# Five norms of a two-layer trunk: two units of weights multiplied before the root is known

## What is computed

```python
h = modulate(rms_norm(x), sh, sc)      # x * rsqrt(mean(x*x) + EPS) * (1 + sc) + sh
x = x + 0.5 * g[:, None, :] * swiglu(h, w_gu, w_down)   # or g * mixer(h)
def swiglu(h, w_gu, w_down):
    g, u = jnp.split(h @ w_gu, 2, axis=-1)
    return (jax.nn.silu(g) * u) @ w_down
```

## Times and profile before

| | us |
|---|---|
| median of 3 runs | 2059.26 (2059.01 to 2061.18) |
| the profiled execution | 2060.86 |
| its span | 2059.1 |
| PE, matmuls | 2019.0 busy, 98% of the span |
| PE, weight loads | 1668.5, 81% |
| DVE | 1084.0, 53% |
| ACT | 683.8, 33% |
| POOL | 185.3, 9% |

### The profile page before, as it was taken

One profiled execution on the slowest core, in us unless ns is written; L12 is line 12 of the kernel. 1 busy time (PEld: TensorE's weight loads), 2 busy tenths in 40 slices (PEclk: granted clock), 3 DMA queues, 4 the chain that ended last, 5 costly groups with the idle time before them and its releaser, 6 DMA issues.

```text
span 2059.1 us, 23630 instructions
## 1 busy us (share of the span) xinstructions
PE 2019.0 (98%) x9290; PEld 1668.5 (81%) x9290; DVE 1084.0 (53%) x1642; ACT 683.8 (33%) x986; POOL 185.3 (9%) x216
## 2 busy tenths in 40 slices
PE   6999999999999999999999999999999999999998
PEld 5888888788888888887888888878888878888886
DVE  7665653579746655635654553365455453433334
ACT  5222222344633322224222221345454443222122
POOL 3110100016600101000110000000000000000000
PEclk9999999999999999999999999999999999999999
DMA  8665642322035656523454542221222123322321
GB/s 325 230 212 173 201 145 70 95 86 72 21 103 173 205 172 203 184 85 95 147 189 137 164 153 92 72 93 60 74 71 62 52 82 102 103 92 92 102 87 57
DMA packets 72014, 253.98 MB, mean 123 GB/s; under 512 B 8025, under 2 KB 8153, under 8 KB 71938
## 3 DMA queue, kind: packets, MB, share of 16 engines
q1 hardware_dynamic: 53280, 185.62, 27.7%
q0 software_dynamic: 18512, 67.26, 10.0%
q10 hardware_dynamic: 146, 0.09, 0.0%
HBM read 250.70 MB, written 2.10 MB: 123 GB/s over the span
## 4 chain that ended last, share of the span: by engine, by line
PE 93%; DVE 4%; ACT 1%; issue 1%; POOL 1%; ACTq 0%; DVEq 0%; POOLq 0%
PE bank L1125 28%; PE bank L1130 28%; PE bank L1126 28%; PE bank L1187 1%; PE bank L1136 1%; DVE arena L951 1%; DVE top L950 1%; PE bank L1501 1%; PE bank L1538 1%; PE bank L1430 1%; PE bank L1271 1%; DVE wlo L665 1%; PE bank L1273 1%; PE bank L1272 0%; PE bank L1489 0%
## 5 line engine op out<-in xcount | busy, mean ns | idle before, releaser
L1125 PE MATMUL bank<-h_hi,whi 128*128 128x512 f32 x1808 | 711.0, 393 | 9.5 <-DVE wlo L665 4.5
L1126 PE MATMUL bank<-h_hi,wlo 128*128 128x512 f32 x1808 | 705.8, 390 | 0.0
L1130 PE MATMUL bank<-h_lo,whi 128*128 128x512 f32 x1808 | 589.6, 391 | 0.5 <-POOL h_lo L311 0.5
L382 ACT ACTIVATE whi<-wraw 128x1024 fp32r<-128x1024 f32 x338 | 346.8, 1055 | 269.1 <-PE bank L1130 266.1
L665 DVE TENSOR_TENSOR wlo<-wraw,whi 128x1024 fp32r<-128x1024 f32 x325 | 390.2, 1224 | 55.7 <-ACT whi L382 54.2
L1125 PEld LDWEIGHTS bank<-h_hi,whi 128*128 128x128 f32 x1808 | 340.8, 188 | 83.9 <-issue 11.0
L1130 PEld LDWEIGHTS bank<-h_lo,whi 128*128 128x128 f32 x1808 | 338.9, 188 | 75.2 <-DVE h_lo L740 3.4
L1126 PEld LDWEIGHTS bank<-h_hi,wlo 128*128 128x128 f32 x1808 | 340.8, 189 | 69.7
L1130 PE MATMUL bank<-hid_lo,whi 128*128 128x512 f32 x832 | 324.3, 390 | 3.2 <-DVE hid_lo L793 3.2
L788 DVE TENSOR_TENSOR dve_tmp<-act_tmp,bank 128x512 f32<-128x512 f32 x88 | 60.6, 689 | 504.3 <-ACT act_tmp L429 504.2
L1125 PE MATMUL bank<-hid_hi,whi 128*128 128x512 f32 x832 | 324.6, 390 | 0.0
(11 more groups left out here) (207 smaller groups left out, 1348.7 us busy)
## 6 DMA issues: line engine op xcount, KB each, us to landing
wraw<-in_w_units_dram SPq DMA_DIRECT2D x306, 512.0 KB, 3.5
arena<-in_mod_t_dram POOLq DMA_DIRECT2D x96, 512.0 KB, 4.9
mod_tile<-in_mod_t_dram POOLq DMA_DIRECT2D x32, 512.0 KB, 4.6
wraw<-in_w_units_dram SPq DMA_DIRECT2D x32, 384.0 KB, 3.3
arena<-in_mod_t_dram SPq DMA_DIRECT2D x12, 512.0 KB, 7.9
xT<-in_xt_dram SPq DMA_DIRECT2D x8, 256.0 KB, 4.0
out_dram<-xT SPq DMA_DIRECT2D x8, 256.0 KB, 2.2
mod_tile<-in_mod_t_dram SPq DMA_DIRECT2D x2, 512.0 KB, 9.5
```

The costliest lines, as they stand in the source:

```text
L382: act.activation(whi[:, s % RING, :, :], wraw[:, s % RING, :, :], ACT.Copy).then_inc(hi_ready, 1)
L1125: pe.matmul(dst, whi[:, w, k, :], hi_, start=first, stop=False)
L1126: pe.matmul(dst, wlo[:, w, k, :], hi_, start=False, stop=False)
L1130: return pe.matmul(dst, whi[:, s % RING, k, :], lo_, start=False, stop=last)
```

## The change

Behind each of the five norms the first two units no longer read h. They read the scaled residual x (1 + sc), split into the same `h_hi` and `h_lo`, made by ACT and DVE in `down_stats` as each xT[d] is ready. PE's new `early` runs these two units one after the other, with the sums of squares behind the fourth k-step of the first, the spread of the root behind its eighth (norm 3: the second spread behind the fourth k-step of the second unit), and two more matmuls in each k-step: the weight tile's high and low part by the shift, split in two columns (`shift_split`), into bank 5. ACT copies the spread root from RB to `ssum`. DVE's `take_early` sums the parts of sh W, multiplies both units' banks by the root into `sq`, and the shift enters as a bias or scalar at the next instruction. h itself is made as before, but each piece overwrites the scaled residual's only when the second unit has used it, and is read from the third unit on. All fillers at the five norms are gone; the last norm's stay. In FoX the forget sums and the bias matmuls move behind head 0's first work, and the layer-0 final scaling of xT (`post_first`) moves into FFN 2. The core of the diff:

```diff
+            def round_h(st, s):
+
+                v, sh, _ = modulation(st)
+                act.wait_ge(rb_ready, RB_BEFORE[v])
+                act.activation(ssum[:, :], bank[RB], ACT.Copy).then_inc(rb_kept, 1)
                 for k in range(KT):
+                    if k == 3:
+                        hi(s + 4)
+                    if k == 7:
+                        hi(s + 5)
+                    act.wait_ge(early_used, KT * (v - 1) + k + 1)
...
+                            if early and q == 0:
+                                act.wait_ge(evicted, s + 1)
+                                act.activation(act_tmp[:, 0, :], sq[:, 0, :], ACT.Silu, bias=shift_out[:, 0:1],
+                                               scale=1.0).then_inc(act_out, 1)
+                                act.wait_ge(early_gated, f)
+                                act.activation(hid_hi[:, bass.ds(h0, 1), :], dve_tmp[:, 0:1, :], ACT.Copy)\
+                                    .then_inc(hid_rounded, 1)
+                                continue
...
+                    if st in NORM:
+                        v, _, column = modulation(st)
+                        if d == 0:
+                            act.wait_ge(shift_ready, v)
+                        act.activation(h_hi[:, d, :], xT[:, d, :], ACT.Copy, scale=column[:, d:d + 1])\
+                            .then_inc(early_rounded, 1)
...
+            def early_lower(st, d):
+
+                v, _, column = modulation(st)
+                dve.wait_ge(early_rounded, KT * (v - 1) + d + 1)
+                dve.scalar_tensor_tensor(out=h_lo[:, d, :], in0=xT[:, d, :], scalar=column[:, d:d + 1],
+                                         in1=h_hi[:, d, :].bitcast(F32), op0=ALU.mult, op1=ALU.subtract)\
+                    .then_inc(early_ready, 1)
...
+            def early_shift(s):
+
+                dve.wait_ge(unit_done, s + 2)
+                parts = bank[SHIFT_BANK][:, 0:4].rearrange("p (u c) -> p u c", u=2)
+                link(dve.tensor_copy(shift_out[:, :], parts[:, :, 0]))
+                link(dve.tensor_tensor(shift_out[:, :], parts[:, :, 1], shift_out[:, :], ALU.add))
+
+            def early_ffn(s):
+
+                early_shift(s)
+                for q in range(2):
+                    dve.tensor_tensor(sq[:, q, :], bank[(s + q) % 4], ssum[:, :], ALU.mult).then_inc(evicted, 1)
...
+            def early_fox(s):
+
+                early_shift(s)
+                link(dve.tensor_tensor(sq[0:HEADS, 0, :], bank[EARLY_BANK[4][0]][0:HEADS, :], ssum[0:HEADS, :], ALU.mult))
+                dve.tensor_tensor(sq[:, 1, :], bank[EARLY_BANK[4][1]], ssum[:, :], ALU.mult).then_inc(early_scaled, 1)
...
+                    if k == 4:
+                        lo(s + 4)
+                    if k == 5:
+                        take_early(s)
...
-            norm(3, 3, 1, 0, fused=True)
-            for d in range(KT):
-                dve.scalar_tensor_tensor(out=xT[:, d, :], in0=xT[:, d, :], scalar=gains[:, d:d + 1],
-                                         in1=bank[POST_RB][:, :], op0=ALU.mult, op1=ALU.mult).then_inc(posted, 1)
-            dve.wait_ge(posted, KT)
+            norm(3, FFN_BASE[2], early_ffn)
...
+            def forget_sums():
+                link(dve.memset(sq[0:HEADS, 0, :], 1.0))
+                dve.wait_ge(ls_ready, 2)
+                link(dve.scalar_tensor_tensor(out=z, in0=z, scalar=0.0, in1=z_small, op0=ALU.min, op1=ALU.subtract))
+                link(dve.tensor_tensor_scan(cum[0:HEADS, :], sq[0:HEADS, 0, :], z, 0.0, ALU.mult, ALU.subtract))
+                link(dve.tensor_copy(cum_hi, cum[0:HEADS, :]))
+                dve.tensor_tensor(cum_lo, cum[0:HEADS, :], cum_hi.bitcast(F32), ALU.subtract).then_inc(cum_ready, 1)
...
-                keep_warm(8, st)
+
+            def stat_spread(st, dst):
+
                 pe.wait_ge(root_ready, ROOTS_BEFORE[st] + 1)
-                spread(bank[POST_RB if st == 3 else RB], NORM_JOB[st], 0).then_inc(rb_ready, 1)
-                if st == 3:
-                    keep_warm(8)
-                    pe.wait_ge(root_ready, ROOTS_BEFORE[4] + 1)
-                    spread(bank[RB], NORM_JOB[4], 0).then_inc(rb_ready, 1)
-                keep_warm(6, st)
...
+            def early(s, st):
+
+                v = NORM[st][0]
+                banks = EARLY_BANK.get(v, (s % 4, (s + 1) % 4))
+                pe.wait_ge(shift_ready, v)
+                for q in range(2):
+                    pe.wait_ge(lo_ready, s + q + 1)
+                    pe.wait_ge(evicted, s if q else s - 2)
+                    w = (s + q) % RING
+                    for k in range(KT):
+                        at = KT * (v - 1) + k + 1
+                        if q == 0:
+                            pe.wait_ge(early_rounded, at)
+                        with_hi(bank[banks[q]], s + q, k, h_hi[:, k, :], k == 0)
+                        if q == 0:
+                            pe.wait_ge(early_ready, at)
+                        ins = with_lo(bank[banks[q]], s + q, k, h_lo[:, k, :], k == KT - 1)
+                        if q:
+                            ins.then_inc(early_used, 1)
+                        for m, weights in enumerate((whi, wlo)):
+                            ins = pe.matmul(bank[SHIFT_BANK][:, 2 * q:2 * q + 2], weights[:, w, k, :], shift_split[:, k, :],
+                                            start=(q == k == m == 0), stop=(k == KT - 1 and m == 1), skip_group_check=True)
+                        if k == KT - 1:
+                            ins.then_inc(unit_done, 1)
+                        if k == 3 and q == 0:
+                            stat_sums(st)
+                        if k == 3 and q and st == 3:
+                            pe.wait_ge(root_ready, ROOTS_BEFORE[4] + 1)
+                            spread(bank[RB], NORM_JOB[4], 0).then_inc(rb_ready, 1)
+                    if q == 0:
+                        stat_spread(st, POST_RB if st == 3 else RB)
...
+                section(n + 1, bank[(n + 1) % 2], 0, KT, h_hi, h_lo, None, None if j else 4)
...
+            keep_warm(3)
+            stat_sums(7)
+            keep_warm(8)
+            stat_spread(7, RB)
```

More of the change, by code:

```diff
@@ L501, in iq_unit @@
                 act.activation(hid_hi[:, n, :], bank[(U + n + 1) % 2], ACT.Copy).then_inc(iq_rounded, 1)
-                for m in range(count):
-                    hi(U + 4 + n + m + (1 if n else 0))
+                if count:
+                    hi(U + 5 + n)
             def relus(g):
@@ L778, in down_stats, with post_first @@
                         lo(down + d + 3)
+                    if d and st in NORM:
+                        early_lower(st, d - 1)
+                if st in NORM:
+                    early_lower(st, KT - 1)
+            def post_first(d):
+                dve.scalar_tensor_tensor(out=xT[:, d, :], in0=xT[:, d, :], scalar=gains[:, d:d + 1],
+                                         in1=bank[POST_RB][:, :], op0=ALU.mult, op1=ALU.mult).then_inc(posted, 1)
             def ffn(f, st):
@@ L891, in _ @@
             ffn(0, 1)
-            norm(1, 1, 0, 1)
+            norm(1, DSA_BASE, early_dsa)
             U = DSA_BASE
@@ L1228, in up_body @@
                             s = up + 2 * q
-                            pair(s, i, (s % 4, (s + 1) % 4), s - 2, v if first and q == 0 else None)
+                            if first and q == 0:
+                                early(s, st)
+                            else:
+                                pair(s, i, (s % 4, (s + 1) % 4), s - 2, v if first else None)
                     if t == 0:
@@ L1435, in dsa_out @@
                 if k0 == 0:
-                    begin(U + 17 + d, U + 17 if d < 4 else U + 14 + d)
+                    before = [e for e in range(d) if DSA_OUT[e] == DSA_OUT[d]]
+                    begin(U + 17 + d, U + 18 + before[-1] if before else U + 17)
                 section(U + 17 + d, bank[DSA_OUT[d]], k0, k1, hid_hi, hid_lo, HID_BASE["dsa"])
```

219 lines of the change are left out of this document (134 added, 85 removed).

## The result

The changed kernel took 2047.05 us (median of 4 executions, 2044.81 to 2048.36), against 2059.14 (2057.74 to 2061.18) for the kernel before beside it: the ratio is 0.9939, 95% interval 0.9922 to 0.9957. It is faster by 12 us, 0.6%. The forecast was 2073, slower; the time lies in the range, near the first rival's. The profiled execution took 2046.44 us, its span is 2044.6 against 2059.1, so 14.5 shorter.

The account below looks back on a forecast made before the run. TensorE's row of wide matmuls was taken as the bound, with 58.8 us of gaps at five norms to win. Clock held, -19.9 gave 2039.4; clock falls added 33.5, making 2073 us, range 2039 to 2088.

Parts of the forecast that it names:

- first rival: At the norms, the clock holds or comes back after one short stretch: 2039 to 2045 us, chance 0.30.
- sum with the clock held: Whole kernel at 2.4 GHz: gaps removed, narrow matmuls and waits added, -19.9 us, giving 2039.4.
- the row of FoX: Sixteen narrow one-column matmuls in FoX, taken as the price of the early units' narrow matmuls: 0.112 us each.
- DVE's margin of 1 us: Norm 2's early units: DVE finishes its pieces about 1 us before the pair needs them, so nothing waits.
- rival 2: Clock holds but DVE's margin fails at five norms, 1 to 3 us each: 2045 to 2054, chance 0.05.
- the clock term: Early units behind the five norms: expected falls to half clock add 33.5 us, making 2073.
- the clock stays low until the plain pair: Early units: once fallen, half clock lasts until plain wide matmuls; 10.6 us per fall at norms 1, 2, 5.
- the mixture of a k-step: Early units at half clock: 1.28 us wide work in 1.71, about the earlier trace's mixture that stayed low.
- norm 3 surely, the others with 0.6: Clock falls at the five norms: certain at norm 3, chance 0.6 at each other, 3.4 of 5 expected.
- norm 4's waits: Norm 4 and FoX: +3.9 us for fresh h from DVE, +1.7 for scores behind the forget sums.
- The forecast's own range: Time if the clock falls at two or more norms and stays low: 2060 or 2062 to 2088, chance 0.55.
- The floor of 25 ns: Skill's gap between narrow matmul starts: 160 shift matmuls would cost 4.0 us, not 17.9; results 14 us lower.

Follow-up runs that it names:

- shift_three: Changed kernel with three two-column shift matmuls in each k-step instead of two, the third into columns nobody reads: 2074.72 us, ratio 1.0071 to the kernel before.
- shift_twice: Changed kernel with each k-step's two shift matmuls done twice, the second time into columns nobody reads: 2116.05 us, ratio 1.0278 to the kernel before.
- late_split_rows: Changed kernel with two-column shift stationary, norm 3's sums in two groups, norm 4's extra vector work behind h's last piece: 2036.14 us, 0.9891 of before.
- no_fill: Kernel before without its filler matmuls at the five norms, the last norm's kept: 2069.56 us, ratio 1.0048 to the kernel before.

## Why the prediction was wrong

**The sum with the clock held was right to 3 us.** The falls seen cost about half their length: 3.4 at norm 3 and 1.7 each in DSA, norm 4 and FoX, 8.5 together, so that with the clock held -14.5 would be -23.0, for -19.9. The -14.5 is between two traced executions; the medians are 12.1 apart, by which it would be -20.6. By parts: norm 1 up to DSA's first index scores went from 424.42 - 389.33 = 35.09 to 418.84 - 389.72 = 29.12, -6.0, and the part to norm 2 is -3.9 - 1.7 = -5.6, as forecast. Norms 2 and 5, without a fall, gave -4.0 and -4.1 for -3.8, and the early stretch is 17.27 for 17.3. The narrow matmuls cost what the row of FoX had promised, 0.112 (0.110 and 0.104 to 0.112 in two experiments). Norm 3 is -3.7 - 3.4 = -7.1 for -6.4, since `h_lo` is waited for 1.2 and not 2.5. Norm 4 is 0.8 - 3.4 = -2.6 for -0.3: the waits are 2.5 and 0.8 for 3.9 and 1.7. DVE's margin of 1 us held, so rival 2 fell.

**The step that failed is the clock term**, and in it the sentence that the clock stays low until the plain pair, 10.6 us a fall. In the trace of after the clock came back in the middle of the early units. PE's timeline at norm 3:

```profile
977.36 0.77 PE L1244 MATMUL bank<-h_hi,whi 128*128 128x512 f32 x1
...
979.07 0.78 PE L1244 MATMUL bank<-h_hi,whi 128*128 128x512 f32 x1
...
980.77 0.74 PE L1244 MATMUL bank<-h_hi,whi 128*128 128x512 f32 x1
```

A k-step took 1.71 at half clock, as the forecast had said, and within the third behind the sums the clock was back (at 981.35). The forecast had taken the mixture of a k-step for the one of the earlier trace rows, which stayed low. But that row is no mixture of three and two. PE's timeline of the kernel before, in it:

```profile
982.64 3.76 PE L1136 MATMUL bank<-hid_hi,ident_r 128*128 128x512 f32 x8
986.21 1.97 PE L1187 MATMUL bank<-ident_r,root 128*128 128x128 f32 x8
987.98 3.72 PE L1136 MATMUL bank<-hid_hi,ident_r 128*128 128x512 f32 x8
```

Here stand two runs of eight fillers, the end of a row of narrow sums, and rows of eight 128-column spreads. An average over 10 us of it said nothing on how the clock would take a finer mixture. Nor is it so simple that wide matmuls back to back bring the clock back: the first eight fillers, from 982.64 to 986.21, did not, where eight at norm 2 had the earlier trace rows. `shift_three` and `shift_twice` show where the described course begins: with one or two narrow matmuls more in a k-step eight of the nine falls at the norms in their two traces lasted 24 to 34 us, and one 13.65.

**How often it falls** was not far off. Forecast: norm 3 surely, the others with 0.6, so 3.4 of 5. The two profiles of the changed kernel have falls at norms 3 and 4, and at norms 2, 3 and 4. The term that was mis-sized is the price of one: 1.7, and 3.4 at norm 3, instead of 8 to 10.6. The forecast's own number of falls at this price is 2.4 x 1.7 + 3.4 = 7.5 instead of 33.5, and 2039.4 + 7.5 = 2046.9 for a measured 2047.05. That this fits so closely is luck: the two falls in DSA and behind norm 4, 3.4 together, are not in it, norm 4's waits were 2.3 less than forecast, and executions of one kernel differ by 3 us. The forecast's own range, too, stands at 2060 in one place and at 2062 in the other; neither reaches down to the measured time. That the time lies in the stated range of 2039 to 2088 is because the range was drawn over the first rival too. Its first rival had named this course, "fallen clock recovers inside unit 1", and was given 0.30 and 2039 to 2045; the measured time is 2 us above it.

TensorE: Matmul & The Clock Gate (the Trainium skill, section "Why this matters for your kernels") ties a fall to idle gaps between bursts of matmuls. The trace agrees in part. Two of the four falls stand behind gaps (PE busy 0.86 of 3.42 us ahead of DSA's, 1.63 of 3.47 ahead of the one behind norm 4), and the direction that the section gave, no long loss without a gap, was right for this kernel. As the only cause it does not hold here: ahead of norm 3's fall PE was busy 3.41 of 3.41 us and ahead of norm 4's 6.29 of 6.29, and in `shift_twice` the clock stayed low for 34.13 busy us. The same page's section "LDWEIGHTS (loading the stationary operand)" gives a load's time as its columns over 1.2 GHz, an estimate of 107 ns for 128 columns. At full clock the runs agree: 110 ns with 128 stationary columns. With two, 128 moving columns took 60. At half clock a load is dearer, which that figure doesn't tell: two narrow matmuls added 1.71 - 3 x 0.43 = 0.42 us to a k-step, 0.21 each. The floor of 25 ns, by which every result of the prediction would have been 14 lower, is not reached with such a load.

**What stays open.** DSA's fall at 513 is in every profile but those of before and `late_split_rows`, in `no_fill`'s too, which has none of the early units; PE's wait on `rowmax` ahead of it was 2.57 us in the trace of before as well. So the change need not be its cause, which wasn't tested. It costs some 1.7, an estimate by half its length. The clock also stands low at the end of the last norm in every profile, for 2.5 us in that of before and 5.2 to 14.5 in the others, and what that costs was measured nowhere. Nor does any run tell why norm 5 of `shift_twice` kept its clock where norms 1, 2 and 4, with the same k-steps, did not, or why the clock falls at norms 2 and 4 in some executions of one kernel and not in others. And `qk`'s wait of 0.8 behind the forget sums was left as it is.

## What to carry to other kernels

Fill the gap behind a reduction with real work whose result can be corrected afterwards: fillers only keep the clock, the chain behind the gap gets no shorter by them, and a row of them in front of it can hold it up (1.1 us at norm 2). Price a narrow matmul by its stationary columns, and put the small operand there, if the layout allows; then look for who has to wait for the result, since PE's own gain of 8.2 us gave 5.3. When a clock fall that comes and goes stands in one trace and not in the other, read its price out of the difference before the edit gets the credit. Where the clock decides the sign, an average row of a stretch with other work in it isn't evidence for the new order: look at how long each kind of instruction runs in a row, and give the course in which a fall is short its own full weight.

## What was not expected of the hardware

The clock has two courses at one and the same instruction stream: in `shift_twice` 26.00 us at 1.00 at norm 5, and 27.30 at 0.50 with the same k-steps at norms 1, 2 and 4. One and two narrow matmuls more per k-step, 0.11 us each, moved the kernel by 28 and 69 us, mostly through the clock; and a matmul of 128 moving columns with two stationary ones took 0.06 us where one of two moving columns with 128 stationary took 0.11.
